# New feed-forward orders on VectorE, ScalarE and TensorE in a decoder-step kernel

## The chip, the cores and the metric

One NeuronCore of one Trainium2 chip runs the whole program. The metric is the device time of one execution in microseconds (us). The time before is the median of three executions.

## What is computed

One inference step of a two-layer decoder trunk: an HGRN2 layer, then a stick-breaking attention layer with a shared K/V, each followed by the same kind of feed-forward layer. Width is 1024, inner width 4096, and there are 576 tokens (512 of a prompt, 64 of eight samples). All in float32. The change touches the feed-forward layers alone:

```
def sq_relu_mlp(xn, w_up, w_down):
    h = jax.nn.relu(xn @ w_up)
    return (h * h) @ w_down
...
h = h + sq_relu_mlp(rmsnorm(h, g_mlp[l]), w_up[l], w_down[l])
```

## The kernel before, in words

**Three products for one.** A float32 product is made of three faster ones. Each operand is split in a high part (a rounded copy, made by ScalarE) and a low part (the operand less its high part, made by VectorE): high times high, high times low, low times high.

**Quads.** The weights of a feed-forward layer come in panels of 1024 by 256. Such a panel and the 576 tokens form one *quad*, G. Its 2 by 2 blocks are multiplied in the manner of Strassen: `N_PC` = 7 products instead of 8, so that sums and differences of blocks of both operands are needed. Every product is 4 depths of 128 times 3 parts, 12 matmuls of 288 columns, so a quad is 84 matmuls. `PRODUCT` gives for product 0 to 6 the PSUM bank (A, C, B, A, D, C, A) and which slot of the moving operand it takes. Banks C and B are added to, A is used three times in a quad, and so A must be copied out between its uses.

**Order of the quads** (`quad_order`). The inner width is cut in `FCH` = 4 chunks. `place(G)` = (layer, chunk c, r): r = 0 to 3 are up quads (input times w_up), r = 4 to 7 down quads (hidden times w_down). After quad (0, 0) the order of a chunk is r = 1, 2, 3, then r = 0 of the next chunk, then r = 4, 5, 6, 7. In the text below these are U1, U2, U3, U0, D4, D5, D6, D7. This period of eight is run three times in each of the two layers; what is left is a last chunk without U0 (U1, U2, U3, D4 to D7 in the first layer; U1, U2, U3 in the second, whose last down products are made in the plain way, without Strassen, in `panel`). There are 32 + 28 = 60 quads.

**The weights of quad G.** SyncE loads the panel with two DMAs (`raw_panel`, L493). GpSimd issues three more in `weight_sums`: a copy of one block column (L692), and two that add a block while they load (L695 a row sum, L697 a column sum). ScalarE makes the high parts: `raw_high` (L820), `sums_high` (L837), `corner_high` (L828), `last_sums_high` (L847). VectorE makes two more sums, `sum_three` (L1919) and `sum_all` (L1929), and the low parts: `raw_low` (L1934), `sums_low` (L1940), `corner_low` (L1944), `last_sums_low` (L1949). High and low parts have one buffer each: `raw_high(G + 1)` waits until product 2 of quad G has been made, `sums_high` for product 3, `corner_high` for product 4, `last_sums_high(G + 1)` for the end of quad G.

**What an up quad leaves to do.** ScalarE copies the banks A, C, A, D out (`copy_out`, L887). VectorE adds and subtracts banks (`add_first` L2081, `add_second` L2089) and applies relu times the norm (`relu_pair`, L2112). ScalarE squares (`square_pair`, L895). The result is a pair of hidden blocks, an operand of the down quads: VectorE makes three differences of its blocks (L1955, L1961, L1966), ScalarE the high parts (`blocks_high`, `differences_high`, L852), VectorE the low parts (`blocks_low` 128x864, `differences_low` 128x1152, both L1979). All of it for the pair of quad G - 1 stands in the order of quad G, but `add_first(G)`, which closes quad G. In a down quad VectorE adds the banks to the residual instead, in six parts (`h_part_1` to `_6`, L2162, L2181, L2188).

**What sets the order.** Every engine runs its own list, written out by hand per quad in `up_quad` and `down_quad`, and takes nothing out of order. TensorE goes through the products in `quad`, in `first_down` for D4 (`op_lo` counts the operand's low parts: depths 0 to 2 of D4 need `base + 6`, depth 3 needs `blocks_low` of U3, which is `base + 7`, and `differences_low` of U3, `base + 8`), in `first_quad` for quad 0 of a layer and the D4 of the last chunk of the first layer. `product` waits for the weights' low parts (`piece_lo`), `bank_ready` for the bank: product 3, 5 and 6 for the copies of this quad, product 0 for `add_second` of quad G - 2, products 1 and 2 for `add_first` of quad G - 2.

## Time and profile before

| | |
|---|---|
| Median of three executions | 1570.16 us (1568.03 to 1574.05) |
| The profiled execution | 1566.42 us, its span 1564.6 us |
| TensorE busy | 1495.1 us, 96% |
| VectorE busy | 1198.2 us, 77% |
| ScalarE busy | 823.1 us, 53% |
| GpSimd busy | 338.2 us, 22% |
| Granted TensorE clock, mean | 0.993 |
| DMA | 205.83 MB, mean 132 GB/s |

Busy time of TensorE is modelled: a matmul is shown with some 295 ns from its start to its end, while the next one starts 133 ns after it. A gap of TensorE shows in the idle column as soon as it is longer than what is left of the matmul before it, and the true loss is some 0.16 us more than that column says. The two feed-forward layers lie between 379 and 768 us and between 1157 and 1499 us of the span.

### The profile page before, as it was taken

The page shows a single profiled execution, that of the slowest core. Times are in us where ns is not written, and L with a number is a line of the kernel's source. Part 1 is how long each engine was busy: PE and PEld are TensorE (multiplying, and loading weights), DVE is VectorE, ACT ScalarE, POOL GpSimd, SP SyncE. Part 2 cuts the span into 40 slices and gives each one's busy share as a digit, 9 for nine tenths or more (in the row PEclk, how much of TensorE's full clock was granted, in tenths as well). Part 3 has the DMA queues.
Part 4 walks back from the last instruction along what each step waited for, and adds up shares of the span by engine and source line. Part 5 has one row for each costly group of instructions (what it writes and reads, how often), then busy time and mean ns, then how long its engine had stood idle before and what let it go on. Part 6 is the DMA issues. An engine that isn't in the chain of part 4 may idle for free.

```text
span 1564.6 us, 33777 instructions
## 1 busy us (share of the span) xinstructions
PE 1495.1 (96%) x13024; PEld 1412.7 (90%) x13024; DVE 1198.2 (77%) x1997; ACT 823.1 (53%) x1296; POOL 338.2 (22%) x322
## 2 busy tenths in 40 slices
PE   8999999999989899898899999999999898999988
PEld 8999999989989899898898888888899898998988
DVE  8866666669987979888735888888689889798743
ACT  6444444446644535454434777768656455363533
POOL 3000000003222222232342121111342232222141
PEclk9999999999999999999999999999999999999999
DMA  6233333225767677775325565454257776767611
GB/s 184 54 96 89 87 87 88 84 72 127 154 146 170 146 153 160 160 151 133 96 87 184 192 197 169 149 163 147 73 109 162 160 149 143 178 143 150 154 57 61
DMA packets 237716, 205.83 MB, mean 132 GB/s; under 512 B 8268, under 2 KB 224404, under 8 KB 237588
## 3 DMA queue, kind: packets, MB, share of 16 engines
q1 hardware_dynamic: 151346, 147.34, 29.9%
q0 software_dynamic: 68160, 47.20, 19.9%
q10 hardware_dynamic: 18082, 9.48, 2.2%
q8 instruction: 93, 1.52, 0.4%
q14 instruction: 35, 0.29, 0.1%
HBM read 192.19 MB, written 11.80 MB: 130 GB/s over the span
## 4 chain that ended last, share of the span: by engine, by line
PE 74%; DVE 16%; ACT 5%; issue 5%; DMA 0%; DVEq 0%; ACTq 0%
PE acc L2680 23%; PE acc L3003 10%; PE pL L3003 8%; PE acc L3097 6%; PE pM L3003 5%; PE pM L3155 3%; DVE H_lo L1979 2%; DVE H_f L2112 2%; DVE lo L1934 2%; PE pO L3003 2%; ACT H_f L895 1%; PE acc L2941 1%; PE pL L2801 1%; ACT hi L820 1%; DVE lo L1940 1%
## 5 line engine op out<-in xcount | busy, mean ns | idle before, releaser
L637 POOL TENSOR_TENSOR wlo<-wraw,whi 128x512 fp32r<-128x512 f32 x48 | 69.0, 1467 | 464.6 <-ACT whi L751 464.6
L2680 PE MATMUL acc<-xa_hi,whi 128*128 128x288 f32 x544 | 126.0, 313 | 3.4 <-issue 3.4
L1934 DVE TENSOR_TENSOR lo<-wraw,hi 128x1024 fp32r<-128x1024 f32 x60 | 73.5, 1226 | 70.1 <-ACT hi L820 70.1
L3003 PE MATMUL acc<-X_hi,hi 128*128 128x288 f32 x384 | 114.4, 298 | 4.6 <-DVE lo L1940 4.4
L2680 PE MATMUL acc<-xa_hi,wlo 128*128 128x288 f32 x544 | 117.4, 297 | 0.0
L2680 PE MATMUL acc<-xa_lo,whi 128*128 128x288 f32 x544 | 117.1, 297 | 0.0
L3003 PE MATMUL acc<-H_hi,hi 128*128 128x288 f32 x336 | 100.5, 299 | 15.4 <-DVE H_lo L1979 15.4
L3003 PE MATMUL acc<-X_lo,hi 128*128 128x288 f32 x384 | 113.3, 295 | 0.0
L3003 PE MATMUL acc<-X_hi,lo 128*128 128x288 f32 x384 | 113.1, 295 | 0.0
L837 ACT ACTIVATE hi<-wraw 128x1024 fp32r<-128x1024 f32 x60 | 63.7, 1062 | 82.9 <-DVE wraw L1919 80.2
L820 ACT ACTIVATE hi<-wraw 128x1024 fp32r<-128x1024 f32 x60 | 63.4, 1056 | 78.3 <-PE acc L3003 78.3
L3003 PE MATMUL acc<-H_lo,hi 128*128 128x288 f32 x336 | 99.9, 297 | 0.0
L3003 PE MATMUL acc<-H_hi,lo 128*128 128x288 f32 x336 | 99.7, 297 | 0.0
L705 POOL TENSOR_TENSOR wlo<-wraw,whi 128x512 fp32r<-128x512 f32 x36 | 49.9, 1407 | 217.6 <-ACT whi L1264 190.2
L2680 PEld LDWEIGHTS acc<-xa_hi,whi 128*128 128x128 f32 x544 | 86.7, 191 | 10.5 <-issue 8.1
L2680 PEld LDWEIGHTS acc<-xa_hi,wlo 128*128 128x128 f32 x544 | 88.3, 190 | 0.0
L2680 PEld LDWEIGHTS acc<-xa_lo,whi 128*128 128x128 f32 x544 | 87.9, 190 | 0.0
L3003 PE MATMUL pL<-X_hi,hi 128*128 128x288 f32 x256 | 75.9, 296 | 8.0 <-ACT H_f L887 8.0
L3003 PEld LDWEIGHTS acc<-H_hi,hi 128*128 128x128 f32 x336 | 63.6, 189 | 17.5 <-DVE H_lo L1979 17.3
L3003 PEld LDWEIGHTS acc<-X_hi,hi 128*128 128x128 f32 x384 | 72.0, 187 | 6.8 <-DVE lo L1940 6.7
L3003 PE MATMUL pL<-X_lo,hi 128*128 128x288 f32 x256 | 75.6, 295 | 0.0
L3003 PE MATMUL pL<-X_hi,lo 128*128 128x288 f32 x256 | 75.5, 295 | 0.0
(547 smaller groups left out, 5149.4 us busy)
## 6 DMA issues: line engine op xcount, KB each, us to landing
wraw<-in_w_up_dram SPq DMA_DIRECT2D x64, 512.0 KB, 4.9
wraw<-in_w_down_dram SPq DMA_DIRECT2D x64, 512.0 KB, 4.5
Kp<-in_cache_k_dram SPq DMA_DIRECT2D x32, 512.0 KB, 4.2
Vp<-in_cache_v_dram SPq DMA_DIRECT2D x32, 512.0 KB, 5.4
wraw<-in_w_in_a_dram SPq DMA_DIRECT2D x30, 512.0 KB, 5.6
S_even<-in_w_up_dram POOLq DMA_DIRECT2D x32, 256.0 KB, 4.7
wraw<-in_w_up_dram POOLq DMA_DIRECT2D x32, 256.0 KB, 4.8
S_odd<-in_w_up_dram POOLq DMA_DIRECT2D x32, 256.0 KB, 5.5
```

What stands on the lines that cost most here:

```text
L637: ins = pool.tensor_tensor(wlo[s][:, k:k + 2, :], wraw[s][:, k:k + 2, :], whi[s][:, k:k + 2, :].bitcast(F32), ALU.subtract)
L705: ins = pool.tensor_tensor(wlo0[:, k:k + 4, cols], wraw0[:, k:k + 4, cols], whi0[:, k:k + 4, cols].bitcast(F32), ALU.subtract)
L820: act.activation(blocks4(hi02), by_rows(G % 2)[:, 0], ACT.Copy).then_inc(piece_hi, 1)
L837: act.activation(blocks4(hi31), by_depth(G % 2)[:, 0], ACT.Copy).then_inc(piece_hi, 1)
L895: act.activation(v, v, ACT.Square).then_inc(squared, 1)
L1934: dve.tensor_tensor(blocks4(lo02), by_rows(G % 2)[:, 0], blocks4(hi02).bitcast(F32), ALU.subtract).then_inc(piece_lo, 1)
L1979: dve.tensor_tensor(lo, full, hi.bitcast(F32), ALU.subtract).then_inc(op_lo, 1)
L2112: ins = dve.scalar_tensor_tensor(out=v, in0=v, scalar=0.0, in1=r, op0=ALU.max, op1=ALU.mult)
L2680: last = pe.matmul(acc[a][:, hf, 0:HALF], w[s][:, k, a * P:(a + 1) * P], x[k][:, hf * HALF:(hf + 1) * HALF], start=(k == 0 and n == 0), st ...
L3003: last = pe.matmul(out, w[i][:, k, :], x[:, k, slot, :], start=(k == 0 and m == 0 and i in (0, 1, 2, 4)), stop=(k == 3 and m == 2), skip_g ...
L3097: last = pe.matmul(acc[0][:, hf, 0:HALF], w[:, k, a * P:(a + 1) * P], x[:, k, hf * HALF:(hf + 1) * HALF], start=(k == 0 and m == 0), stop= ...
L3155: last = pe.matmul(pM[:, c:c + w], (tri_r if k2 == kb else ones_r)[:], u[:, UOFF[k2]:UOFF[k2] + w], start=(k2 == kb and u is uh[hh]), stop ...
```

## The change

- **VectorE, up quads.** `add_first(G - 1)` moves from the end of quad G - 1 to the head of quad G. `corner_low` moves from the quad before to its own quad. The three differences of a pair are taken apart and put between `sum_three`, `sum_all` and `sums_low`, and are made in the quad right after the pair's. The low parts of that pair are made one quad later than they were (`pair_two_before`); the pair of U0 is held until the next U1 (`pair_held`).
- **VectorE, down quads.** D4 gets `blocks_low` and `differences_low` of U3 and the additions of U0, D6 the relu of U0. `sum_all` of D5 is made in D5 and not in D4. `h_part_5` moves to the quad after its own.
- **ScalarE.** Bank copies come before the square; `raw_high` comes before the square; `blocks_high` of the last pair is put at the end of the quad, its `differences_high` at the head of the next one. The square of U0 moves from D4 to D6.
- **TensorE.** D4 goes through depths 0 to 2 of products 0, 2 and 1 before it waits for depth 3.
- The D5 to D7 of the first layer's last chunk keep the old order under a new name, `last_down`.

The operations are the same, and as many. The core of the diff:

```diff
+        def pair_before(G):
+            return place(G - 1) if G not in (0, N_Q0) and is_up(G - 1) else None
+        def last_pairs(G):
+            return place(G)[1] == FCH - 1 and place(G)[2] > 1
+        def pair_two_before(G):
+            if G % N_Q0 < 2 or not (is_up(G - 1) and is_up(G - 2)) or plain(*place(G - 2)[0:2]) or last_pairs(G):
+                return None
+            return place(G - 2)
+        def pair_held(G):
+            n, c, r = place(G)
+            return (n, c, 0) if r == 1 and c else None
...
 # ScalarE
             def up_quad(G, call=None):
                 last_sums_high(G)
+                if before is not None:
+                    differences_high(*before)
+                if split_held:
+                    blocks_high(*held)
                 copy_out(G, "A", 0, 1)
-                if evac:
-                    square_pair(G - 1)
                 copy_out(G, "C", 3, 2)
-                if pair is not None and not plain(*pair[0:2]):
-                    blocks_high(*pair)
                 if more:
                     raw_high(G + 1)
-                if pair is not None and not plain(*pair[0:2]):
-                    differences_high(*pair)
+                if behind is not None:
+                    square_pair(G - 1)
                 copy_out(G, "A", 1, 4)
+                if split_held:
+                    differences_high(*held)
                 if more:
                     sums_high(G + 1)
                 copy_out(G, "D", 2, 5)
                 if more:
                     corner_high(G + 1)
...
+                if behind is not None and not plain(*behind[0:2]):
+                    blocks_high(*behind)
+                    if last_pairs(G):
+                        differences_high(*behind)
...
+            def first_down(G):
+                last_sums_high(G)
+                differences_high(*place(G - 2))
+                raw_high(G + 1)
+                sums_high(G + 1)
+                corner_high(G + 1)
+            def down_quad(G):
+                last_sums_high(G)
+                raw_high(G + 1)
+                if place(G)[2] == 6:
+                    square_pair(G - 3)
+                sums_high(G + 1)
+                corner_high(G + 1)
...
 # VectorE
             def sums_low(G):
-                dve.wait_ge(sums, 2 * G + 2)
+                dve.wait_ge(sums, 2 * G + 1)
...
             def up_quad(G):
-                if evac:
+                if behind is not None:
+                    add_first(G - 1)
+                    if before is not None:
+                        blocks_low(*before)
                     add_second(G - 1)
+                    corner_low(G)
                     relu_pair(G - 1)
-                elif c:
+                elif held is not None:
+                    h_part_5(G - 1)
                     h_part_6(G - 1)
+                    corner_low(G)
                 last_sums_low(G)
-                if split:
-                    differences(*pair)
+                if before is not None:
+                    differences_low(*before)
+                if split_held:
+                    differences(*held)
+                    blocks_low(*held)
                 if more:
                     raw_low(G + 1)
+                if split:
+                    difference_13(*behind)
+                if more:
                     sum_three(G + 1)
+                if split:
+                    difference_2(*behind)
+                if more:
                     sum_all(G + 1)
                 if split:
-                    blocks_low(*pair)
+                    difference_4(*behind)
+                if split_held:
+                    differences_low(*held)
                 if more:
                     sums_low(G + 1)
-                add_first(G)
-                if more:
-                    corner_low(G + 1)
-                if split:
-                    differences_low(*pair)
+                if split and last_pairs(G):
+                    blocks_low(*behind)
+                    differences_low(*behind)
...
+            def first_down(G):
+                corner_low(G)
+                blocks_low(*place(G - 2))
+                differences_low(*place(G - 2))
+                h_part_1(G)
+                last_sums_low(G)
+                h_part_2(G)
+                raw_low(G + 1)
+                h_part_3(G)
+                add_first(G - 1)
+                sum_three(G + 1)
+                add_second(G - 1)
+                h_part_4(G)
+                sums_low(G + 1)
+            def down_quad(G):
+                h_part_5(G - 1)
+                h_part_6(G - 1)
+                corner_low(G)
+                if r == 5:
+                    sum_all(G)
+                h_part_1(G)
+                if r == 6:
+                    relu_pair(G - 3)
+                last_sums_low(G)
+                h_part_2(G)
+                raw_low(G + 1)
+                h_part_3(G)
+                sum_three(G + 1)
+                h_part_4(G)
+                sum_all(G + 1)
+                sums_low(G + 1)
...
 # TensorE
             def first_down(G):
                 base = op_base(made(*place(G)[0:2]))
                 pe.wait_ge(op_lo, base + 6)
-                product(G, 0, 0, 3)
+                for i in (0, 2, 1):
+                    product(G, i, 0, 3)
                 pe.wait_ge(op_lo, base + 7)
                 product(G, 0, 3, 4).then_inc(product_done, 1)
+                product(G, 2, 3, 4)
+                product(G, 4, 0, 3)
                 pe.wait_ge(op_lo, base + 8)
-                for i in range(1, N_PC):
+                product(G, 1, 3, 4).then_inc(product_done, 2)
+                product(G, 3, 0, 4).then_inc(product_done, 1)
+                product(G, 4, 3, 4).then_inc(product_done, 1)
+                for i in (5, 6):
                     product(G, i, 0, 4).then_inc(product_done, 1)
```

## Rows read from the trace of the kernel before

**Rows 1.** The page: busy us (share of the span) xinstructions.
```profile
PE 1495.1 (96%) x13024; PEld 1412.7 (90%) x13024; DVE 1198.2 (77%) x1997; ACT 823.1 (53%) x1296; POOL 338.2 (22%) x322
```
**Rows 2.** What TensorE waited for in one period of eight quads, 449.35 to 545 us.
```profile
PE acc L3003 <- DVE H_lo L1979: 2.6, 1, 2.6
PE pL L3003 <- ACT H_f L887: 1.1, 1, 1.1
PE pM L3003 <- ACT H L887: 1.1, 1, 1.1
```
**Rows 3.** Busy time by engine: a period, an up quad's turn, a down quad.
```profile
449.35:545.00 95.65, 90.50 (x673) 89.42 (x673) 82.32 (x109) 46.43 (x61) 26.62 (x25) 1.00 0.71 155
412.57:425.38 12.81, 12.81 (x97) 12.66 (x96) 12.16 (x16) 7.82 (x12) 3.52 (x4) 1.00 0.65 146
467.11:478.27 11.16, 11.16 (x87) 11.16 (x86) 8.45 (x13) 3.70 (x4) 3.32 (x3) 1.00 0.61 145
```
**Rows 4.** VectorE's instructions in order of time, one turn of an up quad.
```profile
412.57 1.23 DVE L1934 TENSOR_TENSOR lo<-wraw,hi 128x1024 fp32r<-128x1024 f32 x1 [0.31 <-ACT hi L820]
413.90 0.69 DVE L1919 TENSOR_TENSOR wraw<-wraw 128x512 f32<-128x512 f32 x1
414.62 0.69 DVE L1929 TENSOR_TENSOR S_odd<-wraw 128x512 f32<-128x512 f32 x1
415.23 1.05 DVE L1979 TENSOR_TENSOR H_lo<-H_f,H_hi 128x864 fp32r<-128x864 f32 x1
416.20 1.22 DVE L1940 TENSOR_TENSOR lo<-wraw,hi 128x1024 fp32r<-128x1024 f32 x1
417.34 0.75 DVE L2081 TENSOR_TENSOR H_f<-H_f,acc 128x576 f32<-128x576 f32 x1
418.00 0.69 DVE L1944 TENSOR_TENSOR lo<-wraw,hi 128x512 fp32r<-128x512 f32 x1
418.60 1.35 DVE L1979 TENSOR_TENSOR H_lo<-H_f,H_hi 128x1152 fp32r<-128x1152 f32 x1
419.87 0.75 DVE L2089 TENSOR_TENSOR H_f<-H_f,pM 128x576 f32<-128x576 f32 x1
420.65 1.43 DVE L2112 SCALAR_TENSOR_TENSOR H_f<-H_f,rstd 128x576 f32<-128x576 f32 x2
422.00 1.22 DVE L1949 TENSOR_TENSOR lo<-S_odd,hi 128x1024 fp32r<-128x1024 f32 x1
423.32 0.76 DVE L1955 TENSOR_TENSOR H_f<-H_f 128x576 f32<-128x576 f32 x1
424.11 0.46 DVE L1961 SCALAR_TENSOR_TENSOR H_f<-H_f 128x288 f32<-128x288 f32 x1
424.60 0.46 DVE L1966 TENSOR_TENSOR H_f<-H_f 128x288 f32<-128x288 f32 x1
```
**Rows 5.** ScalarE in the same turn: its square, behind relu.
```profile
422.12 1.17 ACT L895 ACTIVATE H_f<-H_f 128x1152 f32<-128x1152 f32 x1 [4.12 <-DVE H_f L2112]
```
**Rows 6.** Quad D5: its first matmul, `raw_high` and `raw_low` for D6, a later addition.
```profile
455.79 0.29 PE L3003 MATMUL pM<-H_hi,hi 128*128 128x288 f32 x1
...
460.84 1.06 ACT L820 ACTIVATE hi<-wraw 128x1024 fp32r<-128x1024 f32 x1 [3.71 <-PE acc L3003]
...
461.93 1.23 DVE L1934 TENSOR_TENSOR lo<-wraw,hi 128x1024 fp32r<-128x1024 f32 x1 [2.30 <-ACT hi L820]
...
466.23 0.45 DVE L2162 TENSOR_TENSOR hT<-hT,pO 128x288 f32<-128x288 f32 x1
```
**Rows 7.** The last D4 of the first layer: TensorE's longest wait in it.
```profile
719.77 0.40 PE L3003 MATMUL pM<-H_hi,hi 128*128 128x288 f32 x1 [3.36 <-DVE H_lo L1979]
```
**Rows 8.** Busy time and granted clock (0.53) just after that wait.
```profile
720.60:722.60 2.00, 2.00 (x11) 2.00 (x10) 1.21 (x2) 1.97 (x4) 0.00 (x0) 0.53 1.08 379
```
**Rows 9.** DMA to landing, all of L493 (SyncE's panels).
```profile
DMA to landing us min/median/max: 3.4/4.6/7.1
```
**Rows 10.** DMA to landing, all of L695 (GpSimd's row sums).
```profile
DMA to landing us min/median/max: 4.3/4.8/6.2
```

More of the change, by code:

```diff
@@ L978, in up_quad, with steady_quads, last_down @@
                     corner_high(G + 1)
[L979 to L980 removed]
+                if behind is not None and not plain(*behind[0:2]):
+                    blocks_high(*behind)
+                    if last_pairs(G):
+                        differences_high(*behind)
+                elif behind is not None:
+                    plain_high(*behind)
+                elif held is not None and not split_held:
+                    plain_high(*held)
                 if call is not None:
                     norm_rstd(call)
[L984 to L986 removed]
+            def first_down(G):
                 last_sums_high(G)
[L988 to L992 removed]
+                differences_high(*place(G - 2))
[9 more added lines that the diff above has]
+                corner_high(G + 1)
+            def steady_quads(g0, g1):
+                for G in range(g0, g1):
+                    if is_up(G):
+                        up_quad(G)
+                    elif place(G)[2] == 4:
+                        first_down(G)
+                    else:
+                        down_quad(G)
+            def last_down(G, blocks, nxt=None):
+                last_sums_high(G)
+                blocks(0)
+                blocks(1)
                 if nxt is None:
@@ L1220, in _ @@
             up_quad(0, n_norm["mlp0"])
-            for G in range(1, N_Q0 - 4):
-                if is_up(G):
-                    up_quad(G)
-                else:
-                    down_quad(G)
+            steady_quads(1, N_Q0 - 4)
             def first_query_panel():
@@ L2125, in up_quad @@
                 n, c, i = place(G)
-                evac = G not in (0, N_Q0) and is_up(G - 1)
-                pair = (n, c, i - 1) if i else (n, c - 1, 3) if c else None
-                split = pair is not None and not plain(*pair[0:2])
                 more = G + 1 < (N_Q0, N_Q0 + N_Q1)[n]
-                last = i == 3 and c == FCH - 1
-                if evac:
+                behind, before, held = pair_before(G), pair_two_before(G), pair_held(G)
+                split = behind is not None and not plain(*behind[0:2])
@@ L2153, in up_quad @@
+                if i == 3 and c == FCH - 1:
+                    add_first(G)
+                    if more:
+                        corner_low(G + 1)
                     relu_half(G, 0)
-                if pair is not None and not split:
+                if behind is not None and not split:
                     hidden_low(2 * i - 2)
                     hidden_low(2 * i - 1)
+                elif held is not None and not split_held:
+                    hidden_low(0)
+                    hidden_low(1)
@@ L2234, in down_quad @@
                     sum_all(G + 1)
-                if m0 is not None:
-                    query_low(m0)
+                query_low(m0)
                 h_part_3(G)
@@ L2240, in down_quad @@
                 h_part_4(G)
-                if m0 is not None:
-                    query_low(m0 + 1)
+                query_low(m0 + 1)
                 h_part_5(G)
@@ L2245, in down_quad, with steady_quads @@
                     corner_low(G + 1)
+            def steady_quads(g0, g1):
+                for G in range(g0, g1):
+                    if is_up(G):
+                        up_quad(G)
+                    elif place(G)[2] == 4:
+                        first_down(G)
+                    else:
+                        down_quad(G)
             enter_mlp(0, U_OUT, n_norm["mlp0"])
```

73 lines of the change are left out of this document (28 added, 45 removed).

## The prediction

> **What bounds the kernel now.** I read four views, from coarse to fine.
>
> The page shows TensorE busy for 96% of the span and VectorE for 77% [rows 1]. Read alone it says that TensorE is the bound and an order on other engines can't matter. But a busy TensorE is not one at its pace, so I looked at how long a quad takes. A down quad takes 11.16 us [rows 3]: 84 matmuls, one every 0.133 us, with no gap. That is the floor, and eight quads would take 8 x 11.16 = 89.28 us. The period of eight takes 95.65 us [rows 3]. So 6.37 us are lost in each period, six times in the kernel: 38.2 us.
>
> The waits say where [rows 2]: 2.6 us for an operand's low part (D4 waits for U3's differences), 1.1 us twice for a bank copy (in U3 and in U0). Each is 0.16 us more in truth, in all 5.3 of the 6.37 us; the rest are slivers. None is in D5 to D7 or U1.
>
> The cause is in VectorE's list [rows 4]. From one `raw_low` to the next is 12.81 us in an up quad (412.57 to 425.38), 1.65 us over the floor, and VectorE is busy for 12.16 of them [rows 3]. In a down quad it is busy for 8.45 of 11.16 and waits 2.30 us before `raw_low` [rows 3, 6]. So **VectorE bounds the up quads and TensorE the down quads**; over a period VectorE needs only 82.32 of 95.65 us. The copies are late because ScalarE stands 4.12 us before its square [rows 5], with copies queued behind, until a late VectorE has made relu.
>
> **The change part by part.** My sum is for the profiled execution.
>
> *VectorE's turn in an up quad.* From start to next start rows 4 give: raw 1.33, sum_three 0.72, sum_all 0.61, blocks_low 0.97, sums_low 1.14, add_first 0.66, corner 0.60, differences_low 1.27, add_second 0.78, relu 1.35, last_sums 1.32, the differences 0.79, 0.49 and 0.78. An instruction that needs nothing of the one before starts some 0.08 us before that one's end (sum_all lasts 0.69 and the next starts at 0.61), one that needs it 0.03 us after (sum_three lasts 0.69, sum_all starts at 0.72). The new order puts another instruction between nearly all such pairs. Raw becomes 1.14, sum_three 0.61, add_second 0.67, last_sums 1.14, the differences 0.68, 0.38, 0.38 (the last one loses its wait for `raw_high`, which now precedes the square). That is 1.21 us less: **11.60 us** for U3 and U0. U2 has no pair two before it, so 0.97 + 1.27 less: **9.36**. So two of the four quads are 0.44 us over the floor and one is 1.8 under.
>
> The Trainium skill (VectorE: DVE Perf Modes, "The DRAIN you can't avoid") says that the next instruction does not start until the pipe is empty and that a semaphore between two costs nothing extra. By it the interleaving would save nothing and an up quad would keep about 12.5 us. The rows differ: 0.61 against 0.72 behind instructions of one length [rows 4]. I go by the rows; the other outcome is rival B.
>
> *When must it be ready.* `raw_high(G + 1)` can start 5.05 us into quad G (455.79 to 460.84) and `raw_low` 6.14 us into it [rows 6]. I count the end of `sums_low(G + 1)` from the start of quad G + 1; TensorE needs it there at 1.60 (product 1), in the new D4 at 2.4 (18 matmuls). For U2: `raw_low` at 6.14, then sum_three, sum_all, differences_low of the held pair, sums_low, 5.1 us in all: 11.2, that is 0.05. U2's own list reaches `raw_low` at 4.5, waits until 6.14 and ends its `sums_low` at about -0.1 of U3. Then +0.44 a quad: 0.4 for U0, 0.8 for D4. All are inside 1.60: **the stalls in U3 and U0 go**.
>
> *ScalarE.* It works 7.82 us in an up turn [rows 3] and keeps its instructions. Copies A and C now stand before the square, so they follow the banks; `raw_high` too. The square runs at 6.1 to 7.3 into the quad, relu ends at 4.6 at the latest. Behind it is the third copy, at 7.6, which product 6 needs at 9.57. `sums_high` waits for sum_three (ends 9.5 in U0) and costs VectorE nothing, since three instructions (1.37 us) stand between. `blocks_high` of the last pair ends at 0.3 to 1.1 in the next quad, the differences' high part by 3.3 in D4.
>
> *D4.* VectorE: corner from 0.8 to 1.4, blocks_low to 2.4, wait until 3.3, differences_low to 4.7. TensorE needs the first at 3.6 (27 matmuls) and the second at 5.6 (42 matmuls), so the wait of 2.73 us goes. What is late next: h_part_1 (5.0; product 3 wants it at 6.0), last_sums 6.1, h_part_2 at 6.3, `raw_low` for D5 to 8.5 (product_done now jumps to 3 only at 6.3), h_part_3 8.9, add_first and add_second of U0 at 10.9, which D5's first matmul needs at 11.16. That margin is 0.25 us; `sums_low` for D5 ends at 1.4 of D5 against 1.6. I price this knot at **0.4 us a period**, from 0 to 2.
>
> *D5 to D7, U1.* D5 takes corner and sum_all (3.9 into it) before h_part_1 at 4.3, wanted at 4.8. The 2.30 us that VectorE idles in each down quad [rows 6] takes up relu of U0 (1.35 in D6), and U1 the differences and blocks_low. Nothing on TensorE's path.
>
> *Queues.* `corner_low` releases SyncE's next panel. In a down quad it comes some 0.6 us later in TensorE's time than now, in D5 3.4 us later (after sum_all, which SyncE needs as well). From D5 + 3.9: SyncE's two issues 0.4, landing 4.6, the row sum 4.8 [rows 9, 10] is D5 + 13.7, while `sum_three` for D7 wants it at D6 + 8, D5 + 19. With the longest landings (7.1 and 6.2) it is D5 + 17.6. Cost 0. GpSimd's issues keep their order behind `last_sums_low`, at 4.5 to 6.1 into every quad. The moved waits hold up nothing else: what is queued behind them on ScalarE is counted above.
>
> *Edges.* First layer, last chunk: no stall in U3 (1.3 us gained), but in U3 the low parts now stand behind `sums_low` and add_first behind them, so the chain to the last pair starts 0.5 us later against D4's start. TensorE's wait there of 3.36 us [rows 7] is split in two of about 2.7 and 3.0. After that wait the granted clock fell to 0.53 for some 2 us [rows 8], hidden in the chain's next wait. Gain 0.9 us, from -2 (the level of 1.2 GHz once more, with nothing to hide it) to +2. The second layer's last chunk has no stall and no gain; its tail after 1491 us keeps its order.
>
> **The sum.** 6 x (6.37 - 0.4) = 35.8, and 0.9: 36.7 us. 1566.42 - 36.7 = 1529.7. The median of the three runs is 3.74 us above the profiled one; for a median I add that: **1533.5 us**.
>
> **Rivals.**
>
> A, my forecast: the stalls of rows 2 go almost wholly. Chance 0.68.
>
> B, the lag persists. VectorE's instructions gain nothing by being interleaved. By rows 4 the up quads with two pairs then take some 12.7 us (the durations alone sum to 12.75), so U3 and U0 fall 3.1 us behind. U0 waits 0.5, D4 0.8 and 0.55, D5 0.6 for add_second: 2.5 a period in place of 0.4, 12.6 us in all: 1546. For: the margin at D5 is only 0.25 us and the lag in D4 is a sum of 14 instructions. Against: 0.61 against 0.72. Chance 0.22.
>
> C, the debt is only moved. The work of VectorE is the same, 82.32 us a period, and D4 gets blocks_low, differences_low and add_first (2.9 us) for a relu of 1.35. If D4's turn runs 5 us longer than I have it, D5's first product waits for add_second as long as the two places do now, and all of 6.37 comes back: 1566 to 1572. Against: D4's list sums to 9.7 us by rows 4 and 6 (an h_part 0.37). Chance 0.06.
>
> D, slower: the panel comes late. The issue of SyncE's panel now hangs on a `corner_low` in the quad itself and in D5 on sum_all. If landings stretched, `sum_three` would wait for the row sum, all of VectorE with it, and TensorE one for one. The DMA engines are busy for 0.71 of a period [rows 3]. It decides once panel and row sum together take over 14.7 us in D5's case, against 9.4 at the median and 13.3 at the longest [rows 9, 10]. To cost more than the 6.4 us gained and another 1.5 us, they must take 22.6: 6 x 1.5 = 9 us, 1579. Chance 0.04.
>
> **The numbers.** What a measurement can tell from no change is about 0.5%, 7.9 us, so "same" is 1562.3 to 1578. A and B lie far below: 0.90, and a little of C: 0.91 faster. C: 0.05 same. D: 0.04 slower. The range must hold A and most of B: low 1527 is no knot in D4, +2 at the edge, and 2 us of the profiled run's distance gone; high 1549 is B with its edge at -2.
>
> **What would show it.** In the changed profile: the period of eight from 95.65 to 89.3 to 90.3 us; the rows "pL <- ACT L887" and "pM <- ACT L887" gone; VectorE's turn from `raw_low` to `raw_low` 11.6 in U3 and U0; in D4 two starts of 9 matmuls more before any wait, and the wait for L1979 left in the last chunk alone; instead perhaps a wait of some 0.3 us for add_second (L2089) or `sums_low` (L1940) at D5. SyncE's issue in D5 nearly 4 us after D5's start, and no wait of L1919 for a DMA. Wrong would be: an up turn above 12.3 us (B), a wait of over 2 us at D4's end (C), L1919 waiting for a row sum (D), or a period that keeps its 95 us.

## The result, and the profile after

| | before | after |
|---|---|---|
| Median, side by side | 1569.10 us (1565.82 to 1574.05, four runs) | 1527.72 us (1527.24 to 1530.92, four runs) |
| Ratio of the medians | | 0.9736, 95% interval 0.9712 to 0.9759 |
| The profiled execution | 1566.42 us | 1528.13 us, its span 1526.4 us |
| Granted clock, mean | 0.993 | 0.993 |

The change is 2.6% faster. The median lies 5.8 us under the forecast of 1533.5 us and 0.7 us inside the lower end of the range (1527 to 1549). In the before column the fourth run, made beside the new kernel, moved the median from 1570.16 to 1569.10 us.

The page of the kernel after has the same instructions on every engine as rows 1:

```profile
PE 1487.9 (97%) x13024; PEld 1412.7 (93%) x13024; DVE 1181.8 (77%) x1997; ACT 823.4 (54%) x1296; POOL 338.3 (22%) x322
```

TensorE is busy for only 7.2 us less and VectorE for 16.4 us less, although the time fell by 38. So shares of the page say little here; a quad's pace says more. This is one period of eight quads after (the columns are those of rows 3):

```profile
462.35:551.64 89.29, 89.29 (x674) 89.29 (x674) 79.99 (x109) 46.52 (x60) 26.66 (x24) 1.00 0.76 166
```

95.65 us have become 89.29, which is eight times 11.16 [rows 3]: TensorE is at its own pace without a gap. VectorE's busy time fell from 82.32 to 79.99 us, with the same 109 instructions. The DMA share rose from 0.71 to 0.76, since the same bytes pass in less time.

What TensorE still waits for between 380 and 760 us, the whole first feed-forward layer (us in total, times, longest):

```profile
PE pM L3106 <- DVE H_lo L2020: 5.2, 2, 2.7
PE acc L2783 <- issue: 3.4, 1, 3.4
PE acc L3106 <- DVE lo L1981: 2.2, 1, 2.2
PE pM L3106 <- DVE hT L2234: 1.1, 1, 1.1
PE pL L3106 <- DVE hT L2234: 0.4, 1, 0.4
```

The three rows of rows 2 are gone. What is left lies in the last chunk, in the plain panel behind the last quad (L2783) and, the 2.2 us at 383.54, ahead of the layer's second quad, where the kernel before has it too. In the steady periods there is no wait at all.

VectorE's turn of U3, in order of time (L1975 is `raw_low`, L1996, L2002 and L2007 the differences, L1960 and L1970 the sums, L1981 `sums_low`, L2020 low parts of a pair):

```profile
500.21 1.23 DVE L1975 TENSOR_TENSOR lo<-wraw,hi 128x1024 fp32r<-128x1024 f32 x1 [1.60 <-ACT hi L839]
501.35 0.75 DVE L1996 TENSOR_TENSOR H_f<-H_f 128x576 f32<-128x576 f32 x1
502.02 0.69 DVE L1960 TENSOR_TENSOR wraw<-wraw 128x512 f32<-128x512 f32 x1
502.62 0.45 DVE L2002 SCALAR_TENSOR_TENSOR H_f<-H_f 128x288 f32<-128x288 f32 x1
502.99 0.68 DVE L1970 TENSOR_TENSOR S_odd<-wraw 128x512 f32<-128x512 f32 x1
503.60 0.45 DVE L2007 TENSOR_TENSOR H_f<-H_f 128x288 f32<-128x288 f32 x1
503.96 1.22 DVE L1981 TENSOR_TENSOR lo<-wraw,hi 128x1024 fp32r<-128x1024 f32 x1
...
511.74 1.22 DVE L1975 TENSOR_TENSOR lo<-wraw,hi 128x1024 fp32r<-128x1024 f32 x1
...
523.27 1.21 DVE L1975 TENSOR_TENSOR lo<-wraw,hi 128x1024 fp32r<-128x1024 f32 x1
```

From `raw_low` to `raw_low` is 11.53 us twice (forecast 11.60; 12.81 before). The wait of 1.60 us ahead of the first one shows that VectorE is ahead of TensorE when U2 begins: U2 is a short turn, as the working had it (it waits from 4.5 to 6.14 into the quad, 1.64 us). Nearly every instruction starts before the one above it has ended: 502.62 is 0.60 after a `sum_three` of 0.69 us, where rows 4 had 0.72.

D4 and the start of D5, VectorE again; D4's first matmul starts at 527.55 and D5's at 538.73 us:

```profile
527.01 1.21 DVE L1981 TENSOR_TENSOR lo<-wraw,hi 128x1024 fp32r<-128x1024 f32 x1
...
530.51 1.36 DVE L2020 TENSOR_TENSOR H_lo<-H_f,H_hi 128x1152 fp32r<-128x1152 f32 x1 [0.71 <-ACT H_hi L871]
...
537.67 0.75 DVE L2141 TENSOR_TENSOR H<-H,pM 128x576 f32<-128x576 f32 x1
...
538.88 1.22 DVE L1981 TENSOR_TENSOR lo<-wraw,hi 128x1024 fp32r<-128x1024 f32 x1
```

The reader can lay the forecast's dates beside this. `sums_low` of D4 ends 0.67 into D4 (forecast 0.8, wanted at 2.4). The last low part ends 4.32 into it (forecast 4.7, wanted at 5.6). `add_second` of U0 (L2141) ends at 538.42, 0.31 us ahead of D5's first matmul (forecast 0.25). `sums_low` of D5 ends 1.37 into D5 (forecast 1.4, wanted at 1.6). So two margins of about 0.25 us hold the period.

**Where the 38.3 us came from.** Between fixed points of the two traces: the first layer's quads, from the first matmul to the plain panel, went from 394.41 to 374.27 us (20.14 gained), the second layer's from 342.90 to 323.50 us (19.40 gained). The stretch between the layers grew by 0.3 us and the end from the second panel on by 0.9 us (65.07 to 65.98). 20.14 + 19.40 - 0.3 - 0.9 = 38.3.

### The profile page after: what moved, and what is told of

The parts are those of the page before. It is cut to its first block, busy times and chain, and to the rows that moved or that the text cites. A ratio compares the mean times of both kernels' runs of the same rounds, so it can differ in the third digit from the quotient of the medians.

```text
span 1526.4 us, 33777 instructions
## 1 busy us (share of the span) xinstructions
PE 1487.9 (97%) x13024; PEld 1412.7 (93%) x13024; DVE 1181.8 (77%) x1997; ACT 823.4 (54%) x1296; POOL 338.3 (22%) x322
## 4 chain that ended last, share of the span: by engine, by line
PE 92%; DVE 4%; issue 1%; ACT 1%; DMA 1%; DVEq 0%; SPq 0%; ACTq 0%
PE acc L2783 23%; PE acc L3106 18%; PE pL L3106 12%; PE pM L3106 9%; PE acc L3206 6%; PE pO L3106 3%; PE pM L3264 3%; PE acc L3044 2%; PE pL L2904 1%; PE pO L3278 1%; PE pL L3247 1%; PE acc L3321 1%; PE acc L3338 1%; PE pO L3310 1%; PE pM L2973 1%
## 5 line engine op out<-in xcount | busy, mean ns | idle before, releaser
L2783 PE MATMUL acc<-xa_hi,whi 128*128 128x288 f32 x544 | 126.0, 313 | 3.4 <-issue 3.4
L2783 PE MATMUL acc<-xa_hi,wlo 128*128 128x288 f32 x544 | 117.3, 297 | 0.0
L2783 PE MATMUL acc<-xa_lo,whi 128*128 128x288 f32 x544 | 117.2, 297 | 0.0
L1975 DVE TENSOR_TENSOR lo<-wraw,hi 128x1024 fp32r<-128x1024 f32 x60 | 73.3, 1222 | 46.0 <-ACT hi L839 46.0
L2783 PEld LDWEIGHTS acc<-xa_hi,whi 128*128 128x128 f32 x544 | 86.7, 191 | 10.5 <-issue 8.1
L2783 PEld LDWEIGHTS acc<-xa_hi,wlo 128*128 128x128 f32 x544 | 88.3, 190 | 0.0
L2783 PEld LDWEIGHTS acc<-xa_lo,whi 128*128 128x128 f32 x544 | 87.9, 190 | 0.0
L1981 DVE TENSOR_TENSOR lo<-wraw,hi 128x1024 fp32r<-128x1024 f32 x60 | 73.2, 1221 | 5.1 <-ACT hi L856 4.5
```

Source lines behind the costliest of these rows:

```text
L1975: dve.tensor_tensor(blocks4(lo02), by_rows(G % 2)[:, 0], blocks4(hi02).bitcast(F32), ALU.subtract).then_inc(piece_lo, 1)
L1981: dve.tensor_tensor(blocks4(lo31), by_depth(G % 2)[:, 0], blocks4(hi31).bitcast(F32), ALU.subtract).then_inc(piece_lo, 1)
L2783: last = pe.matmul(acc[a][:, hf, 0:HALF], w[s][:, k, a * P:(a + 1) * P], x[k][:, hf * HALF:(hf + 1) * HALF], start=(k == 0 and n == 0), st ...
```

## The experiments

They are cut from the kernel before or from the one after. Ratios are to the kernel before on the same chip, with a 95% interval. "Period" is the time from one D7's `raw_low` to that of the next chunk, read four times in each trace (two per layer); before it is 95.58 to 95.92, after 89.29 to 89.30.

### TensorE's order alone, and all but TensorE's order

The first is the kernel before with the new `first_down` on TensorE and nothing else; the second is the kernel after with the old one:

```diff
                 pe.wait_ge(op_lo, base + 6)
-                product(G, 0, 0, 3)
+                for i in (0, 2, 1):
+                    product(G, i, 0, 3)
                 pe.wait_ge(op_lo, base + 7)
...
```

> The kernel before with TensorE's new first_down alone. Theory A (VectorE's list bounds the up quads, D4's wait is a part by itself): the wait for L1979 in D4 (2.73 us) goes, since differences_low ends 4.26 us into D4 and is wanted at 5.6; but h_part_1 stands behind add_second, relu and last_sums and comes 7.9 us into D4, and product 3 now wants it at 6.0: a wait of 1.9 us in place of 2.73 + 0.42. The waits of 1.1 us in U3 and U0 stay. Period 95.65 to 94.4, six times: 7 us less, about 1562. Rival (the depth order is what brings most of the change): period 93 or less, 1553 or less.

> The changed kernel with the old first_down on TensorE. Theory A: blocks_low of U3 ends 2.1 us into D4 and is wanted at 1.2, differences_low ends at 4.2 and is wanted 0.4 us after that: two waits, 0.95 and 1.65 us, 2.6 us a period, 15.6 us in all, about 1543; the up quads keep 11.16. Rival (D4's low parts could as well be late, other waits hide it): 1530.

**Measured, alone on before:** 1565.52 us, ratio 0.9971 (0.9955 to 0.9986); periods 96.01, 96.00, 94.94, 95.91. TensorE's longest wait between 400 and 690 us (the two for L887 stay, 1.1 us each):

```profile
PE pL L3003 <- DVE hT L2162: 5.6, 3, 1.9
```

The wait for the low parts is gone, and behind it stands one for `h_part_1` (L2162), 1.86 us and 0.16 that the column doesn't show: VectorE reaches it late whatever TensorE does in the meantime. That much was expected, with a period of 94.4 us. Three of the four periods are 1.5 to 1.6 us longer than that, and windows of 5 us behind this wait show why (the columns are those of rows 3; the first from the first period, the second from the only D4 of the six where it went otherwise):

```profile
448.87:453.87 5.00, 5.00 (x26) 5.00 (x27) 4.52 (x7) 2.08 (x3) 3.11 (x3) 0.66 0.58 105
...
1323.66:1328.66 5.00, 5.00 (x36) 4.82 (x37) 4.51 (x7) 2.09 (x3) 3.11 (x3) 1.00 0.62 108
```

The wait is 1.86 us in both. Behind the first the granted clock is 0.66 on the mean of 5 us, that is, for two thirds of it at the level of 1.2 GHz, and 26 matmuls are made; behind the second it stays at 1.00, and 36 are made. The clock fell in five of the six, for 1.1 us each by the periods (96.0 against 94.94) and 1.3 us by the ten matmuls of 0.133 us. At the median 4 us were gained of the 7 expected; between the profiled executions it is nothing (1567.27 against 1566.42 us). In the kernel before, the longer wait of each D4 (2.57 us in this column, six times) has no such fall behind it:

```profile
445.62:450.62 5.00, 4.74 (x34) 4.53 (x35) 4.25 (x7) 2.23 (x2) 1.49 (x2) 1.00 0.61 208
```

**Measured, all but TensorE's order:** 1552.08 us, ratio 0.9881 (0.985 to 0.9912), against the 1543 us expected; periods 92.18, 92.18, 93.47, 92.30.

```profile
PE acc L3106 <- DVE H_lo L2020: 4.2, 3, 1.4
PE pL L3106 <- DVE H_lo L2020: 3.2, 3, 1.3
```

Both pieces of the low parts are late in every D4, since they are now made in D4 itself. With 0.16 us each that is 2.8 us a period (2.6 expected), which all but explains 92.18. The rest of the miss is the clock again. It falls in five places of the two layers, in four of which (384, 445, 1213 and 1305 us) the trace of the kernel after has none. Such a fall costs 1.3 us, by the period of 93.47 that has one. Two D4s with the same pair of waits, 0.95 and 1.41 or 1.42 us, show that it doesn't always come:

```profile
630.92:635.92 5.00, 5.00 (x37) 5.00 (x38) 2.25 (x4) 1.06 (x1) 1.16 (x2) 1.00 0.53 175
...
1306.27:1311.27 5.00, 5.00 (x28) 5.00 (x29) 1.90 (x3) 0.15 (x1) 1.19 (x2) 0.71 0.77 251
```

6 x 2.9 and 4 x 1.3 are 22.6 us, and the two profiled executions are 22.6 us apart (so close by luck, since falls outside the layers are left out). **What follows:** TensorE's order is worth at most 4 us on the old VectorE order and about 23 us on the new one (22.6 between the profiled executions, 24 between the medians). The parts of the change are not additive: moving the low parts into D4 pays only if D4 can begin without them.

### ScalarE's order: taken back, and alone

In the first the square goes back ahead of the copy of bank C and of `raw_high`, on the kernel after; in the second ScalarE gets the new order on the kernel before.

```diff
                 copy_out(G, "A", 0, 1)
+                if behind is not None:
+                    square_pair(G - 1)
                 copy_out(G, "C", 3, 2)
                 if more:
                     raw_high(G + 1)
-                if behind is not None:
-                    square_pair(G - 1)
                 copy_out(G, "A", 1, 4)
```

> The changed kernel, ScalarE's square before the copy of C and before raw_high in the up quads, as it was. Theory A (with VectorE no longer behind, ScalarE's order is worth nothing): relu ends 4.0 to 4.4 us into the quad, so raw_high ends 0.2 us later than raw_low could start, copy C comes at 5.6 and is wanted at 8.0: period 89.3 to 89.6, 1528 to 1530. Rival (copies first is what took the waits of 1.1 us away): they come back in U3 and U0, 2.6 us a period, 1543.

> The kernel before with ScalarE's new order alone in the up quads (copies A and C and raw_high before the square, the third copy behind it, then the pair's high parts). Theory A (VectorE's list bounds the up quads): the wait of 0.31 us before raw_low and 0.1 us behind it go from VectorE's turn, 12.81 becomes 12.4, three turns a period: 1.2 us; the waits of TensorE for the copy (L887) go, but others of nearly the same sum take their place (raw_low or sums_low late), and D4's 2.73 stays. Period 95.65 to 94.4, about 1562, unless the clock falls behind a wait as in the depth order alone. Rival (the late copies were the cause): both waits of 1.3 us go for good, period 93 or less, 1553.

**Measured, taken back:** 1529.32 us, ratio 0.973 (0.9707 to 0.9753); periods 89.29, 89.29, 89.33, 89.30. With VectorE's new list relu comes early enough that the square never holds a copy up. Nothing is lost in the periods. In the last chunk the last D4 has one wait of 4.00 us where the kernel after has 2.56 and 2.66, the clock is at its lower level from 700 to 708 us, and the chunk takes 98.96 us against 97.51.

**Measured, alone on before:** 1578.87 us, ratio 1.0053 (1.0035 to 1.0072): slower, where 1562 us had been expected. The waits of rows 2 for L887 are gone and the later turns shrink to 12.41 us, as expected. But the first turn grows, and D4 waits longer. The periods are 97.86, 96.84, 98.36 and 96.92, where 94.4 had been expected. VectorE at the start of its up quads (L1954 is the first difference, L1933 `raw_low`):

```profile
511.41 0.76 DVE L1954 TENSOR_TENSOR H_f<-H_f 128x576 f32<-128x576 f32 x1 [1.50 <-ACT H_f L895]
513.07 1.22 DVE L1933 TENSOR_TENSOR lo<-wraw,hi 128x1024 fp32r<-128x1024 f32 x1
523.81 0.76 DVE L1954 TENSOR_TENSOR H_f<-H_f 128x576 f32<-128x576 f32 x1
525.48 1.22 DVE L1933 TENSOR_TENSOR lo<-wraw,hi 128x1024 fp32r<-128x1024 f32 x1
```

In the old VectorE order the differences stand ahead of `raw_low`. They need the square, and the square now stands behind `raw_high`. So VectorE waits 1.50 us for the square, and all its list is behind by that. TensorE pays in D4:

```profile
PE acc L3002 <- DVE H_lo L1978: 9.0, 3, 3.0
PE acc L3002 <- DVE lo L1939: 6.5, 7, 1.0
```

3.0 us a D4 where it was 2.6 [rows 2], and new waits for `sums_low`, two or three a period of 0.8 to 1.0 us each. They stand in the place of the two for L887: all waits for VectorE sum to 16.2 us in this stretch (a row of 0.7 is not shown), against 15.3 for all waits in the same view of the kernel before, some 0.3 us more a period. That is the smaller part of what was lost. The larger is the clock. It falls behind the wait of 3.01 us in all six D4s, and in two of them it stays down twice as long, as here, 0.50 on the mean of 5 us:

```profile
545.31:550.31 5.00, 5.00 (x21) 5.00 (x22) 3.90 (x6) 1.16 (x1) 1.50 (x2) 0.50 0.61 203
```

The two periods of over 97 us are those with the longer fall. **What follows:** ScalarE's order alone brings nothing, since its waits only change place, and the fall of the clock behind the one that grew makes it 0.5% slower; on VectorE's old list it can't pay. My expectation had named the clock as the exception, but it looked at ScalarE's queue and forgot that VectorE's old order had a consumer of the square ahead of `raw_low`.

### The differences in one group

```diff
-                if split:
-                    difference_13(*behind)
                 if more:
                     sum_three(G + 1)
-                if split:
-                    difference_2(*behind)
-                if more:
                     sum_all(G + 1)
                 if split:
-                    difference_4(*behind)
+                    differences(*behind)
```

> The changed kernel, the three differences in one piece behind sum_all, not between the sums. Theory A: four more pairs of dependent neighbours cost 0.5 us a turn, an up turn of U3 and U0 is 12.0 in place of 11.53; the lag at D4 grows by 1 to 1.4 us and most of it is inside the margins, D4 and D5 lose 0 to 0.5 us a period: 1528 to 1531. By the Trainium skill (VectorE: DVE Perf Modes, The DRAIN you can't avoid) the turn would stay as it is. Rival (the interleaving carries the gain): turn of 12.5, 2 us or more a period, 1540 or more.

**Measured:** 1534.34 us, ratio 0.9763 (0.9739 to 0.9788), over the 1528 to 1531 expected; periods 89.81 four times. The same stretch of VectorE's list as above, with the same instructions:

```profile
500.87 1.23 DVE L1975 TENSOR_TENSOR lo<-wraw,hi 128x1024 fp32r<-128x1024 f32 x1 [1.60 <-ACT hi L839]
502.20 0.69 DVE L1960 TENSOR_TENSOR wraw<-wraw 128x512 f32<-128x512 f32 x1
502.93 0.69 DVE L1970 TENSOR_TENSOR S_odd<-wraw 128x512 f32<-128x512 f32 x1
503.54 0.75 DVE L1996 TENSOR_TENSOR H_f<-H_f 128x576 f32<-128x576 f32 x1
504.32 0.46 DVE L2002 SCALAR_TENSOR_TENSOR H_f<-H_f 128x288 f32<-128x288 f32 x1
504.82 0.46 DVE L2007 TENSOR_TENSOR H_f<-H_f 128x288 f32<-128x288 f32 x1
505.19 1.22 DVE L1981 TENSOR_TENSOR lo<-wraw,hi 128x1024 fp32r<-128x1024 f32 x1
...
512.97 1.22 DVE L1975 TENSOR_TENSOR lo<-wraw,hi 128x1024 fp32r<-128x1024 f32 x1
```

Where an instruction has to do with what the one above it wrote or read, it starts 0.03 to 0.10 us after that one's end (1.33, 0.73, 0.78 and 0.50 us from start to start); apart, it starts some 0.09 before it (1.14, 0.60, 0.67, 0.37). In the kernel such an instruction has a semaphore wait for its neighbour, so the runs don't separate the dependence from the wait. The turn is 12.10 us in place of 11.53. Of these 0.57 us in each of two turns (1.1 a period), 0.52 shows in the period; the rest fits in the slack ahead of `sums_low`. That is 3.1 of 6.6 us. The other 3.5 are outside the steady periods. In the first chunk of each layer TensorE now waits 0.69 us for `sums_low` (at 428.74 and at 1191.04 us), and the clock falls at 1143 us, where the trace of the kernel after has no fall.

**What follows:** interleaving is a gain by itself, as the prediction took it from rows 4. It speaks against rival B. The page named beside it (Trainium skill, VectorE: DVE Perf Modes, "The DRAIN you can't avoid") says that the next instruction waits until the pipe is empty, but also that one which is not held starts earlier. Here the neighbour that needs the result starts after the end, and the independent one before it.

### Relu of U0 back in D4, and low parts in their own quad

The first moves work into D4, the second takes work out of it. Relu of U0 follows `add_second(G - 1)` in D4 (its square comes in D5). In the other, every pair's low parts are made at the end of the quad in which its differences are:

```diff
 # relu in D4
                 add_second(G - 1)
+                relu_pair(G - 1)
                 h_part_4(G)
...
-                if r == 6:
-                    relu_pair(G - 3)
...
 # low parts in their own quad
             def last_pairs(G):
-                return place(G)[1] == FCH - 1 and place(G)[2] > 1
+                return True
...
...
                 corner_low(G)
-                blocks_low(*place(G - 2))
-                differences_low(*place(G - 2))
                 h_part_1(G)
```

> The changed kernel with the relu of U0 back in D4 (behind add_second) and its square in D5. It tests the knot: sums_low for D5 ends 1.23 us into D5 now and is wanted at 1.6. Theory A (the margin at D5 is 0.4 us, and what goes over it is lost one for one): 1.46 us more in front of it, a wait of 1.1 us a period, period 90.4; 6.6 us, 1535, and a fall of the clock behind one of these waits would cost some 1.7 us each. Rival (D4 has room to spare): period 89.3, 1528.

> The changed kernel, but the pairs' blocks_low and differences_low at the end of the quad that follows the pair's (as the last chunk has it) in place of a quad later, so that D4 has none. Theory A (total work and margins decide, not the place): U2, U3 and U0 each carry 11.6 and wait 0.35 for the high part, 0.8 a quad over the floor; at D4 VectorE is 3 to 3.5 us behind with the low parts, which are wanted at 3.6 and 5.6, and sums_low stands before them: period 89.3 to 90.3, 1528 to 1534. Rival (moving the low parts a quad later is what the gain rests on): sums_low late in U0 and D4, 2 us or more a period, period 91.5 or more, 1541 or more.

**Measured, relu in D4:** 1533.9 us, ratio 0.9768 (0.9746 to 0.979); periods 90.50, 90.50, 90.51, 90.43.

```profile
PE acc L3105 <- DVE lo L1981: 2.9, 3, 1.0
```

One more instruction pair of 1.34 us (519.52 to 520.86 is its step in the turn after) makes each period 1.21 us longer: all but 0.13 us of it comes through. That measures the margin at D5, of which the trace above showed 0.23 us at `sums_low`. There is next to nothing left in D4.

**Measured, own quad:** 1533.91 us, ratio 0.9773 (0.975 to 0.9797); periods 89.95 four times.

```profile
PE pL L3103 <- DVE lo L1984: 1.0, 3, 0.3
PE acc L3103 <- DVE lo L1989: 0.5, 1, 0.5
```

Both came as expected (1535 us and 90.4; 1528 to 1534 us and 89.3 to 90.3). **What follows:** that the low parts are made a quad later, on which much of the diff is spent, is worth 0.66 us a period, 4 us in all, of 4.4 between the profiled executions and 6.2 between the medians. The bulk of the 38 us does not hang on it: VectorE's list would be short enough without.

### The panel issued later

SyncE's next panel waits for `raw_low` in place of the `corner_low` ahead of it, 4 to 5 us later in the quad:

```diff
-                    sp.wait_ge(piece_lo, 4 * (G - 2) + 3)
+                    sp.wait_ge(piece_lo, 4 * (G - 1) + 1)
```

> The changed kernel with SyncE's panel for quad G released by raw_low of quad G - 1 in place of corner_low of quad G - 2: about 4 to 5 us later in every quad (in D5 from 3.84 to 7.6 us into it). It prices the slower rival of the prediction. Theory A (the panel and its row sum had 5 us to spare at the median landing): in D5's case 7.6 + 0.4 + 5.4 + 4.8 = 18.2 us, wanted at 18.7: no wait at the median, some where a landing is long, 0 to 3 us a period, 1528 to 1546. Rival (the transfers are near their limit already): every quad waits, 1 us or more each, 8 us a period, 1575 or more.

**Measured:** 1566.9 us (1565.2 to 1573.07), ratio 0.9981 (0.9962 to 1.0); periods 94.85, 94.47, 93.04, 94.81. The whole gain is gone. VectorE's waits from 400 to 780 us (the first two rows), and the landing of all of SyncE's panels in that kernel:

```profile
DVE wraw L1960 <- DMA wraw<-in_w_down_dram: 14.9, 9, 2.9
DVE wraw L1960 <- DMA wraw<-in_w_up_dram: 13.6, 9, 2.5
```

```profile
DMA to landing us min/median/max: 3.8/6.3/9.9
```

In the kernel after the same views give one wait of `sum_three` (L1960) for a DMA in the two layers, 0.6 us, and these landings of SyncE's panels:

```profile
DMA to landing us min/median/max: 3.4/5.4/9.5
```

before they took 4.6 at the median and 7.1 at the longest [rows 9]; GpSimd's row sums (L714) stayed at 4.8 and rose from 6.2 to 7.4 at the longest [rows 10]. **What follows:** this miss is the most useful. I had expected 1528 to 1546 us, by a slack of over 5 us. A delay of 4 to 5 us, with landings 0.9 us longer at the median, is more than the loads have to spare. Rival D's mechanism is real and near, and at this delay its price is the whole gain: `sum_three` waits for the row sum, and VectorE and then TensorE with it.

### The last chunk: two attempts to go on

Most of what is left to wait for stands in the last chunk of the first layer. One version has `add_first` and the relu of the last pair ahead of the low parts in U3, and TensorE takes depths 0 and 1 of four products in the last D4, then their depth 2, before it waits for depth 3:

```diff
+                last = i == 3 and c == FCH - 1
+                if last and more:
+                    add_first(G)
+                    relu_half(G, 0)
                 if split and last_pairs(G):
                     blocks_low(*behind)
                     differences_low(*behind)
...
+                    pe.wait_ge(op_lo, base + 4)
+                    for i in (0, 2, 1, 4):
+                        product(G, i, 0, 2)
+                    pe.wait_ge(op_lo, base + 6)
+                    for i in (0, 2, 1, 4):
+                        product(G, i, 2, 3)
```

The second is that and `h_part_3` ahead of `query_low` on VectorE.

> The changed kernel with three orders changed at the last D4 of the first layer: in its U3, VectorE closes the quad and makes the first half of relu before the low parts of the pair before; TensorE goes through depths 0 and 1 of products 0, 2, 1, 4, then depth 2, before it waits for depth 3. Theory A (the two waits there, 2.72 and 2.83 us, are one chain from add_first to the last low parts; TensorE's order only splits it): the chain starts 1.2 us sooner, the last chunk (97.5 us from raw_low to raw_low eight quads on) takes 96.3; 1.2 us, 1526.5, less than a measurement tells. Rival (what stands before it sets the end of the waits, not the chain): nothing, or a longer wait for the pair before and with it a fall of the clock, 1530.

> As the last D4 chain, and h_part_3 before query_low in the last D5 to D7 as well. TensorE waits 0.57 and 1.23 us there for h_part_3, which stands behind query_low (0.73) or query_low and add_square (1.4 us): these waits go too, 1.8 us more, last chunk 94.5. In all 3 us: 1525 against 1528.

> The changed kernel once more, beside the last chunk candidate on the same chip: 1528.

**Measured:** 1527.03 us, ratio 0.9717 (0.9693 to 0.9742), for the first; 1526.22 us (1523.19 to 1528.21), 0.9708 (0.969 to 0.9726), for the second; 1528.82 us (1524.84 to 1529.29), 0.9719 (0.9701 to 0.9736), for the kernel after, once more on that chip. The last chunk (`raw_low` to `raw_low` over it) goes from 97.51 to 96.63 and 96.00 us; 96.3 and 94.5 were expected. What holds it is still one long wait, now for `corner_low` (L1985), which stands behind the pair's low parts and behind half of the relu:

```profile
PE pO L3111 <- DVE lo L1985: 2.6, 1, 2.6
```

(the longest wait for VectorE in the second version, 400 to 760 us). **What follows:** VectorE is the bound at this edge in each of the two orders that were run; one with `corner_low` further ahead was not. The second version has the lowest median of all, 2.6 us under the kernel after beside it, but the intervals overlap: it may be 1.5 us better, which its chunk shows, and the totals can't tell.

The second trace of the kernel after shows something that the first doesn't. One of its four periods is 89.94 us long, 0.65 more than the others. In its D4 ScalarE waits for a load by GpSimd, the column sum that `last_sums_high` (L866) reads:

```profile
1377.86 1.06 ACT L866 ACTIVATE hi<-S_odd 128x1024 fp32r<-128x1024 f32 x1 [1.51 <-DMA S_odd<-in_w_down_dram]
```

`differences_high`, VectorE's low part and TensorE (0.38 us in its column, at 1381.42 us) wait behind it. So the loads are near their limit in D4 as well, by a way that rival D doesn't have.

## Why the prediction was right, step by step

**The bound.** "VectorE bounds the up quads and TensorE the down quads": right. With VectorE's turn at 11.53 us the three waits of rows 2 went, and with 0.57 us put back per turn some of it returned.

**VectorE's turn**: 11.60 forecast, 11.53 measured. The steps were those of rows 4; six of the fourteen were one or two hundredths of a us shorter than I took them.

**The dates.** In the period shown every one that I worked out was met within 0.4 us, VectorE's nearly all on the early side (`raw_low` for D5 ends at 8.57, forecast 8.5). "All are inside 1.60: the stalls in U3 and U0 go" held.

**ScalarE, cost 0**: right, but the reason was only half of it. The working says that copies and `raw_high` now follow the banks; taking the square back costs nothing in the periods, so with relu early the copies aren't late in either order. What the working didn't say is that the new ScalarE order needs VectorE's: alone it is slower than before, by the clock that falls behind D4's longer wait.

**The knot in D4 and D5, 0.4 us a period**: this is the term that was mis-sized. It measured 0, so 6 x 0.4 = 2.4 us more were gained. The margins of 0.25 and 0.2 us were there (0.31 and 0.23 measured, 0.13 by putting relu back); I had priced the doubt about them and not the sum, which was positive.

**The edges, 0.9 us**: the layers gained 39.54 us in all, of which 6 x 6.37 = 38.2 are the periods; 1.3 us are the edges, 1.0 in the first layer. The wait of rows 7 was to be split in two of about 2.7 and 3.0 us, and was (2.56 and 2.66, with 0.16 each):

```profile
698.49 0.40 PE L3106 MATMUL pM<-H_hi,hi 128*128 128x288 f32 x1 [2.56 <-DVE H_lo L2020]
...
705.41 0.41 PE L3106 MATMUL pM<-H_hi,hi 128*128 128x288 f32 x1 [2.66 <-DVE H_lo L2020]
```

The clock fell behind the second, as behind the wait of rows 7, to a mean of 0.66 over 5 us; at the level of 1.2 GHz matmuls start 0.24 us apart and not 0.133:

```profile
706.00:711.00 5.00, 5.00 (x24) 4.68 (x24) 4.90 (x9) 1.06 (x1) 1.77 (x2) 0.66 0.05 15
```

**Outside the layers** I had nothing and 1.2 us were lost, 0.9 of them after the second layer's quads, in work that the change leaves alone. Over the profiled execution: 36.7 + 2.4 + 0.4 - 1.2 = 38.3.

**The median.** The greater part of the 5.8 us between forecast and median is no part of the kernel. I added 3.74 us, by which the median of before stood over its profiled run; after, the profiled run is itself 0.4 us over the median. That is 4.1 us, and the profiled run was 1.6 us lower than forecast.

**Queues, cost 0.** SyncE's issue in D5 came where it was put (forecast 3.9 into D5; 542.71 is 3.98):

```profile
542.71 0.92 SPq L512 DMA_DIRECT2D wraw<-in_w_down_dram  x2
```

But the bound behind it was wrong: I took landings as constant, 7.1 us at the longest, and they went to 9.5. My "D5 + 17.6" against 19 would have been D5 + 21.2 with both longest landings of after in one quad. One wait of 0.6 us in the whole kernel says that they don't meet; the late panel shows that a few us more do cost. Rival D deserved more than 0.04, and its threshold of 22.6 us was too high: in the late panel the delay, the landing and the row sum make 15.3 us at the median (4.3 in D5, 6.3 and 4.7), and 3.8 to 5.6 us a period are lost, though there every quad's panel is later and not D5's alone.

**The rivals.** B is out by the turn of 11.53 us and by the grouped differences. The sentence beside it took only half of what the Trainium skill says there (VectorE: DVE Perf Modes, "The DRAIN you can't avoid"): its exception for an instruction that is not held fits the rows. C is out: no wait at D5, though relu in D4 shows how near it was. That D4 pays for everything it is given was right as a mechanism. What was taken back, part by part, is TensorE's order, ScalarE's, the place of the differences, of the low parts and of the relu of U0. No run takes back the moves of `add_first`, `corner_low`, `sum_all` and `h_part_5`, so what each of them is worth stays open.

## What to carry to other kernels

Where one engine bounds some stages and another the rest, give each stage's list as dates against the bound engine's clock; the order that pays is the one in which no date is missed, and its parts can't be priced one by one (ScalarE's order alone is 0.5% slower, TensorE's 0.3% faster, all together 2.6%). On VectorE put an instruction that needs nothing between two that depend on each other: 0.1 to 0.2 us each time here. And after an engine's order has been tightened, the next bound can be a load, as here: the slack of a load is measured by delaying it, not by adding up landings taken from the slower kernel.

## What the runs showed of the hardware

- The granted clock of TensorE falls to the level of 1.2 GHz behind some waits of TensorE of 1 to 3 us, mostly for 3 to 4 us, and a fall costs 1.1 to 1.3 us where a period with one can be laid beside a period without. In the kernel before it stays at 1.00 behind D4's waits of 2.57 us in the periods, yet it falls behind five of six of 1.86 us when TensorE's order alone is changed, and behind all six of 3.01 us when ScalarE's alone is. The same wait of 2.20 us ahead of a layer's second quad has no fall behind it in the trace of the kernel after that is read above (first row), and one in the trace of its second execution (second row):

```profile
383.00:388.00 5.00, 4.46 (x33) 4.47 (x34) 5.00 (x9) 3.35 (x8) 0.00 (x0) 1.00 0.53 165
...
383.00:388.00 5.00, 4.60 (x23) 4.61 (x24) 5.00 (x9) 2.29 (x6) 0.00 (x0) 0.66 0.56 173
```

  So the length of the wait does not decide it, and a sum of gaps came out too low in three of the experiments. What does decide it stays open.
- The landing of one of SyncE's DMAs (half a panel, 512 KB) grew from 4.6 to 5.4 us at the median while the DMA share of a period rose from 0.71 to 0.76, and was 6.3 us when it was issued 4 to 5 us later in the quad, with no more bytes moved. The share alone does not decide it: with relu back in D4 it is 0.76 as well and the median 6.1 us. What it collides with stays open.
